# Split weights of the first expert block, unread PE products and a tail in halves: one change to a hybrid encoder layer with a mixture of experts

## The reference

```python
def finish_layer(x, p, o_attn, c, lp):
    ...
    x = x + mixed
    h = rms_norm(x, lp['g_ffn']).reshape(B * T, D)
    idx, wts = hier_route(h, lp['w_coarse'], lp['b_coarse'], lp['w_fine'], lp['b_fine'])   # 2 of 32 experts
    x = x + moe_ffn(h, idx, wts, lp['w_e_gate'], lp['w_e_up'], lp['w_e_down']).reshape(B, T, D)
    gate = jax.nn.sigmoid(rms_norm(x, lp['g_ple']) @ lp['w_ple_gate'])
    return x + gate * (p @ lp['w_ple_proj'])

# moe_ffn: rows are sorted by expert into blocks of 128; for each block xb of expert e
return (jax.nn.silu(xb @ w_g[e]) * (xb @ w_u[e])) @ w_d[e]
```

## Time and profile before

| | us |
|---|---|
| runs | 1288.11, 1289.12, 1291.49 |
| median | 1289.12 |
| the profiled execution, its own time | 1287.65 |
| its span from the first to the last instruction | 1285.9 |
| PE busy | 1218.7 (95%) |
| DVE busy | 958.7 (75%) |
| ACT busy | 716.3 (56%) |
| POOL busy | 411.0 (32%) |

### The profile page before, as it was taken

One profiled execution on the slowest core, in us unless ns is written; L12 is line 12 of the kernel. 1 busy time (PEld: TensorE's weight loads), 2 busy tenths in 40 slices (PEclk: granted clock), 3 DMA queues, 4 the chain that ended last, 5 costly groups with the idle time before them and its releaser, 6 DMA issues.

```text
span 1285.9 us, 18156 instructions
## 1 busy us (share of the span) xinstructions
PE 1218.7 (95%) x6291; PEld 1015.9 (79%) x6291; DVE 958.7 (75%) x966; ACT 716.3 (56%) x881; POOL 411.0 (32%) x397
## 2 busy tenths in 40 slices
PE   6999988899999999779999999999999999996997
PEld 5887977788788888468888888888888888865886
DVE  5223957788783324879999999999999999975652
ACT  4223325655571221447788777787777777763221
POOL 1000016665141000124554445544455444530000
PEclk9999998999999999989999999999999999998999
DMA  7831001000243220289999999999999999955421
GB/s 257 170 65 37 1 17 61 31 28 1 96 174 130 82 74 29 95 331 368 384 369 384 379 370 364 372 391 380 383 398 389 395 411 403 397 215 196 164 99 49
DMA packets 79487, 287.44 MB, mean 224 GB/s; under 512 B 32848, under 2 KB 35600, under 8 KB 54094
## 3 DMA queue, kind: packets, MB, share of 16 engines
q1 hardware_dynamic: 69214, 268.93, 56.3%
q0 software_dynamic: 10224, 17.85, 3.7%
HBM read 275.60 MB, written 30.60 MB: 238 GB/s over the span
## 4 chain that ended last, share of the span: by engine, by line
PE 54%; DVE 3%; DMA 2%; issue 1%; ACT 1%; POOLq 0%; POOL 0%; SPq 0%; DVEq 0%; ACTq 0%
PE ps L462 16%; PE ps L464 16%; PE ps L463 16%; PE ps L1911 4%; DMA mem<-in_w_e_gate 1%; DVE whl L443 1%; PE ps L2196 1%; PE ps L1918 1%; DMA y_rows<-mem 0%; DMA mem<-y_rows 0%; ACT whl L1220 0%; PE ps L2267 0%; DVE mem L1751 0%; DVE mem L1859 0%; DVE mem L1858 0%
## 5 line engine op out<-in xcount | busy, mean ns | idle before, releaser
L443 DVE TENSOR_TENSOR whl<-mem,whl 128x2048 fp32r<-128x2048 f32 (+2 forms) x216 | 489.5, 2268 | 36.2 <-ACT whl L1220 29.7
L462 PE MATMUL ps<-whl,ahl 128*128 128x512 f32 x1136 | 451.3, 397 | 7.3 <-DVE ahl L443 5.7
L1220 ACT ACTIVATE whl<-mem 128x2048 fp32r<-128x2048 f32 x202 | 387.5, 1919 | 100.0 <-PE ps L464 93.8
L464 PE MATMUL ps<-whl,ahl 128*128 128x512 f32 x1136 | 439.7, 387 | 0.0
L463 PE MATMUL ps<-whl,ahl 128*128 128x512 f32 x1136 | 438.9, 386 | 0.0
L462 PEld LDWEIGHTS ps<-whl,ahl 128*128 128x128 f32 x1136 | 216.7, 191 | 49.4 <-DVE whl L443 3.4
L464 PEld LDWEIGHTS ps<-whl,ahl 128*128 128x128 f32 x1136 | 215.7, 190 | 44.0
L463 PEld LDWEIGHTS ps<-whl,ahl 128*128 128x128 f32 x1136 | 216.3, 190 | 39.8
L892 POOL DMA_INDIRECT y_rows<-mem x35 | 93.8, 2681 | 299.0 <-DVE mem L1805 298.2
L777 POOL TENSOR_SCALAR mem<-mem 128x1 f32<-128x1 f32 (+2 forms) x68 | 20.5, 301 | 396.5 <-ACT mem L968 363.8
L968 ACT ACTIVATE mem<-mem 128x1024 bf16<-128x1024 f32 (+1 forms) x54 | 49.1, 909 | 162.1 <-DVE mem L1702 97.2
(11 more groups left out here) (227 smaller groups left out, 1314.9 us busy)
## 6 DMA issues: line engine op xcount, KB each, us to landing
mem<-in_w_e_gate SPq DMA_DIRECT2D x66, 1024.0 KB, 7.6
mem<-in_w_e_up SPq DMA_DIRECT2D x66, 1024.0 KB, 7.6
mem<-in_w_e_down SPq DMA_DIRECT2D x66, 1024.0 KB, 7.9
mem<-in_x_prompt SPq DMA_DIRECT2D x24, 512.0 KB, 3.5
mem<-y_rows SPq DMA_DIRECT2D x16, 512.0 KB, 5.1
mem<-in_w_in SPq DMA_DIRECT2D x4, 1024.0 KB, 11.8
mem<-in_w_out SPq DMA_DIRECT2D x4, 1024.0 KB, 6.4
h_rows<-mem SPq DMA_DIRECT2D x8, 512.0 KB, 2.6
```

The costliest lines, as they stand in the source:

```text
L443: return which.tensor_tensor(out, full, hi.bitcast(F32), ALU.subtract)
L462: nc.tensor.matmul(out, act_hi, whl[:, 0, w_at], start=first, stop=False)
L464: return nc.tensor.matmul(out, act_lo, whl[:, 0, w_at], start=False, stop=last)
L1220: nc.scalar.activation(whl[:, 0, slot * CH:(slot + 1) * CH], raw[c], ACT.Copy).then_inc(s_mhi, jobs)
```

## The change

Six parts:

1. The high halves of the first expert's four chunks move forward in ACT's queue, around the two exponentials; their low halves move from DVE to POOL, ahead of POOL's first gathers.
2. SP loads chunks 0 to 3 of the second expert between the PLE stores and not behind them.
3. Three of DVE's instructions for the table of spilled blocks (`eb`) move ahead of its wait for the second selection product; the others of that table move behind the index tables. Two buffers change place.
4. `ple_project(4)` moves between the two selection products.
5. PE gets products of the unit matrix by itself into bank 7, which nobody reads (`idle_products`): 19 ahead of the first `slots_turned`, 9 behind it, 26 behind the last expert block and 8 behind the first `x2_transpose`.
6. The last tile of the gate stage is done in two halves of 512 columns: PE makes the whole first half before the second, and tanh, the two DVE products and the store follow by halves.

```diff
@@ SP
             for t in range(Q0, NT):
                 if t + 2 < NT:
                     load_p(t + 2)
                 r = rows_of(t)
+                if t == NT - 3:
+                    load_expert_chunk(1, 1, job(0, 1) + 1)
                 sp.wait_ge(s_convs, 1 + 2 * (t - Q0) + 2)
                 sp.dma_start(Q[t * P:t * P + r], q_out[0:r]).then_inc(s_uos, 16)
+                if t in (Q0 + 1, NT - 3, NT - 2):
+                    c = {Q0 + 1: 0, NT - 3: 2, NT - 2: 3}[t]
+                    load_expert_chunk(1, c, job(0, c) + 1)
...
-            for c in range(4):
-                load_expert_chunk(1, c, job(0, c) + 1)
...
+            for h in range(2):
+                at = slice(h * C, (h + 1) * C)
+                sp.wait_ge(s_3f, NT + h)
+                sp.dma_start(o["y_sample"][0][:, at], fin[TS % 2][0:SAMPLE, at]).then_inc(s_out[TS % 2], 16)
@@ POOL
+            for c in range(4):
+                pool.wait_ge(s_mhi, c + 1)
+                at = slice(c * CH, (c + 1) * CH)
+                lo_part(nc.gpsimd, whl[:, 1, at], whl[:, 0, at], raw[c]).then_inc(s_mlv, 3 if c == 3 else 1)
@@ ACT
+            act.wait_ge(s_w, NT)
+            expert_hi(0, 0, 0, 16, None)
+            act.wait_ge(s_rta, 1)
+            nc.scalar.activation(eqc, dc, ACT.Exp).then_inc(s_rta, 1)
+            expert_hi(1, 1, 1, 16, None)
+            p_turned(2)
+            projected(0)
+            act.wait_ge(s_rta, 3)
+            nc.scalar.activation(e2, mt, ACT.Exp).then_inc(s_rta, 1)
+            expert_hi(2, 2, 2, 16, None)
+            p_turned(3)
+            projected(1)
+            expert_hi(3, 3, 3, 16, None, 3)
...
-            act.wait_ge(s_w, NT)
-            for c in range(4):
-                expert_hi(c, c, c, 16, None, 3 if c == 3 else 1)
-                if c < 2:
-                    p_turned(c + 4)
-                if c < 3:
-                    projected(c + 2)
+            for i in range(2, NQ):
+                if i + 2 < NQ:
+                    p_turned(i + 2)
+                projected(i)
             slots_hi(0, 1)
-            projected(NQ - 1)
...
+            for h in range(2):
+                act.wait_ge(s_3g, NT + h)
+                nc.scalar.activation(tg[TS % 2][:, h * C:(h + 1) * C], bank(2 + 2 * (TS % 2) + h), ACT.Tanh, scale=0.5).then_inc(s_3th, 1)
@@ DVE
+            chain(tt(r3(eb, NE), rowof(start, NOVF), j16, ALU.is_le))
+            chain(tt(r3(eb2, NE), rowof(end, NOVF), j16, ALU.is_gt))
+            chain(tt(eb, eb, eb2, ALU.mult))
             dve.wait_ge(s_rtp, 3)
...
-            expert_lo(0, 0, 0)
             slots_lo(0, 1)
-            expert_lo(1, 1, 1)
-            expert_lo(2, 2, 2)
-            expert_lo(3, 3, 3, 3)
             slots_lo(1, 2)
             gated(1)
             dve.sem_inc(s_hl, 1)
+            dve.wait_ge(s_mlv, 6)
...
+                if t == TS:
+                    dve.wait_ge(s_out[t % 2], 16 * (t // 2))
+                    for h in range(2):
+                        at = slice(h * C, (h + 1) * C)
+                        dve.wait_ge(s_3th, t + h + 1)
+                        nc.vector.scalar_tensor_tensor(tg[t % 2][:, at], tg[t % 2][:, at], 1.0, projected_rows[:, at], ALU.add, ALU.mult).then_inc(s_3m, 1)
+                        dve.wait_ge(s_3m, t + h + 1)
+                        nc.vector.scalar_tensor_tensor(fin[t % 2][:, at], tg[t % 2][:, at], 0.5, R[:, t, at], ALU.mult, ALU.add).then_inc(s_3f, 1)
@@ PE
+            def idle_products(b, n):
+                for i in range(n):
+                    nc.tensor.matmul(bank(b, P), ident, ident, start=(i == 0), stop=(i == n - 1))
...
             for k in range(2):
+                if k == 1:
+                    ple_project(4)
                 pe.wait_ge(s_rt, 3 + k)
...
-            ple_project(4)
             ple_project(5)
             pe.wait_ge(s_tab, 1)
             pe.wait_ge(s_convs, 1 + 2 * (NQ - 1))
+            idle_products(7, 19)
             slots_turned(0, 16, None)
+            idle_products(7, 9)
             pe.wait_ge(s_xsl, 1)
...
+            pe.wait_ge(s_convs, 1 + 2 * NQ + 2)
+            idle_products(7, 26)
...
             x2_transpose(0)
+            idle_products(7, 8)
```

More of the change, by code:

```diff
@@ L187, in build_step @@
         rel = take(NE)
+        eb2 = take(NOVF * NE)
         assert top[0] <= HB0
@@ L191, in build_step @@
         V[0] = take(NT * 2 * NBLK)
-        eb, eb2 = (mem[:, HB0 + i * NOVF * NE:HB0 + (i + 1) * NOVF * NE] for i in range(2))
         assert top[0] <= HT0
@@ L196, in build_step @@
         cmp16 = take(NOVF)
+        eb = take(NOVF * NE)
         assert top[0] <= TAIL
@@ L674, in _, with load_expert_chunk @@
                 sp.dma_start(raw_view(c), expert_chunk(0, c)).then_inc(s_mraw[c], 16)
+            def load_expert_chunk(e, c, lo_before):
+                sp.wait_ge(s_mlv, lo_before)
+                sp.dma_start(raw_view(c), expert_chunk(e, c)).then_inc(s_mraw[c], 16)
             for n in range(2 * NT + 2, 3 * NT):
@@ L758, in _ @@
                     q = t - 3
[L759 to L763, removed]
+                    if q < TS:
+                        sp.wait_ge(s_3f, q + 1)
+                        sp.dma_start(o["y_prompt"][0, q * P:(q + 1) * P], fin[q % 2]).then_inc(s_out[q % 2], 16)
+            for h in range(2):
+                at = slice(h * C, (h + 1) * C)
+                sp.wait_ge(s_3f, NT + h)
+                sp.dma_start(o["y_sample"][0][:, at], fin[TS % 2][0:SAMPLE, at]).then_inc(s_out[TS % 2], 16)
+            sp.wait_ge(s_out[0], 16 * 6)
             sp.wait_ge(s_out[1], 16 * 4)
@@ L1204, in _ @@
                     square_sum(R[:, t, :], junk_of(x1_junk, D), ss1, s_hs)
[L1206 to L1213, removed]
             def expert_hi(J, slot, c, arrived, used, jobs=1):
@@ L1330, in _ @@
                     x2_square(t + 3)
-            act.wait_ge(s_3g, NT)
             act.wait_ge(s_3f, NT - 2)
-            nc.scalar.activation(tg[(NT - 1) % 2], banks2(2 + 2 * ((NT - 1) % 2)), ACT.Tanh, scale=0.5).then_inc(s_3th, 1)
+            for h in range(2):
+                act.wait_ge(s_3g, NT + h)
+                nc.scalar.activation(tg[TS % 2][:, h * C:(h + 1) * C], bank(2 + 2 * (TS % 2) + h), ACT.Tanh, scale=0.5).then_inc(s_3th, 1)
         @block.vector
@@ L1755, in _, with expert_lo @@
                 nc.vector.tensor_tensor(Vv[:, :, 1, :], r3(oh, NBLK), over(wk[k], NBLK), ALU.mult).then_inc(s_rt, 1)
+            def expert_lo(J, slot, c, jobs=1):
+                dve.wait_ge(s_mhi, J + 1)
+                at = slice(slot * CH, (slot + 1) * CH)
+                lo_part(nc.vector, whl[:, 1, at], whl[:, 0, at], raw[c]).then_inc(s_mlv, jobs)
+            j16 = over(iota[:, 0:NOVF], NE)
+            chain(tt(r3(eb, NE), rowof(start, NOVF), j16, ALU.is_le))
+            chain(tt(r3(eb2, NE), rowof(end, NOVF), j16, ALU.is_gt))
+            chain(tt(eb, eb, eb2, ALU.mult))
             dve.wait_ge(s_rtp, 3)
@@ L1767, in _ @@
             nc.vector.tensor_copy(wtab, wts).then_inc(s_tab, 1)
[L1769 to L1782, removed]
             def slots_lo(b, count):
@@ L1805, in out_right @@
                 nc.vector.tensor_scalar(y[:, C:2 * C], bank(6), w_cur[b], None, ALU.mult).then_inc(s_y1, 1)
-            expert_lo(0, 0, 0)
+            chain(tt(r3(eb, NE), r3(eb, NE), rowof(iota[:, 0:NE], NOVF), ALU.mult))
+            chain(red(cmp16, r3(eb, NE), AX.X, ALU.add))
+            chain(nc.vector.tensor_copy(ebk.bitcast(I32), cmp16))
+            nc.vector.tensor_copy(novf.bitcast(I32), end[:, NE - 1:NE]).then_inc(s_tab, 1)
             slots_lo(0, 1)
-            expert_lo(1, 1, 1)
-            expert_lo(2, 2, 2)
-            expert_lo(3, 3, 3, 3)
             slots_lo(1, 2)
@@ L1881, in add_ple @@
                     projected_rows = qb[t % 2]
+                if t == TS:
[6 more added lines that the diff above has]
+                        nc.vector.scalar_tensor_tensor(fin[t % 2][:, at], tg[t % 2][:, at], 0.5, R[:, t, at], ALU.mult, ALU.add).then_inc(s_3f, 1)
+                    return
                 nc.vector.scalar_tensor_tensor(tg[t % 2], tg[t % 2], 1.0, projected_rows, ALU.add, ALU.mult).then_inc(s_3m, 1)
@@ L2405, in _ @@
                     hi, lo = act_tile(t % 2, k)
-                    for i in range(2):
+                    for i in range(2 if t < TS else 1):
                         last = split_product(bank(2 + 2 * (t % 2) + i), hi, lo, slice(k * D + i * C, k * D + (i + 1) * C), k == 0, k == KD - 1)
                 last.then_inc(s_3g, 1)
+            for k in range(KD):
+                hi, lo = act_tile(TS % 2, k)
+                last = split_product(bank(3 + 2 * (TS % 2)), hi, lo, slice(k * D + C, (k + 1) * D), k == 0, k == KD - 1)
+            last.then_inc(s_3g, 1)
 _INS = ['x_prompt', 'x_sample', 'p_prompt', 'p_sample', 'cache_k', 'cache_v', 'state_conv', 'g_mix', 'w_in', 'g_q', 'g_k',
```

3 lines of the change are left out of this document (removed).

## The result

The changed kernel takes 1298.37 us (median of 9 runs, 1292.69 to 1302.66) against 1289.12 us before (9 runs, 1286.62 to 1293.42): a ratio of 1.006, 95% interval 1.0038 to 1.0082. It is slower, by 9.25 us; the forecast was 1298.6.

What follows compares the result with a forecast made beforehand. PE bounds the expert loop; around it, DVE's routing chain and PE's waits decide. Terms 17.0 − 0.3 + 0.65 − 6.0 + 0 − 1.8 = +9.5 us on 1287.65, plus 1.5 for the median: 1298.6; range 1284 to 1305.

Steps and rivals of the forecast that it cites:

- The lock: In the routing, POOL's four 2048-column subtractions, 4.6 us each, hold DVE's two-operand instructions to their end: +17.0 us.
- likeliest case: Whole kernel: POOL's subtractions hold DVE's routing for their whole length; +9.5 us in all, median 1298.6, own range 1292 to 1305.
- Selection products: Two selection products with a PLE product now between them: first at low clock, second at full clock; net −0.3 us.
- First turns: Ahead of the first gathered rows' transposes, PLE product plus 19 idle products fill 7.9 us where 7.24 was: +0.65 us.
- rival 3: DVE is held and idle products run at 1.2 GHz: +4 us ahead of first transposes, +2 at end; 1304, chance 0.12.
- First gate and second block: Expert loop's start: earlier loads −2.6 us, clock kept at first gate −1.7 and at second −1.7; together −6.0.
- Behind the last expert: Idle products in PE's wait after the last expert: −2.4 us if the clock lives, +2.3 if not; taken as 0.
- the case of the lost clock: After the last expert the clock is lost, and the 8 idle products behind the turns run 3.4 us: +2.3 us.
- Tail: Last tile in halves: shorter tanh and two DVE products, −1.5 us, and a half-size store; −1.8 us in all.
- Rival 1: DVE is not held through POOL's long subtractions; copies on ACT delay PE by 1.6 us: −5.9 us, 1283, chance 0.18.
- Rival 4: Half of each POOL subtraction falls on DVE instructions it doesn't hold: +8.5 us instead of 17, 1290, chance 0.11.

Runs made afterwards that it cites:

- e4: Changed kernel with POOL's four subtractions over 1024 columns each, the second half of each low half left out; 1288.50 us in one run.
- e1: Changed kernel with the first expert's low halves back on DVE and the second expert's loads back behind the PLE stores; 1282.74 us, ratio 0.9942 to before.
- e2: Kernel before with only parts 1 and 2 of the change put in; 1305.17 us, ratio 1.0123 to before.
- e7: e6 with idle products resized: 16 for 19, 9 more ahead of the loop, 40 for 26, 4 for 8; 1278.16 us, ratio 0.9907 to before.
- e3: Changed kernel with POOL filling the four chunk buffers with zeros where it subtracted, first expert's low halves left out; 1292.03 us in one run.
- e6: e1 with the second expert's first chunk loaded ahead of the last PLE store, the next three right behind it; 1278.74 us, ratio 0.9913 to before.
- e5: Changed kernel without its four groups of idle products; 782.32 us from last logits to span's end, where the changed kernel has 783.14.
- e8: Changed kernel with POOL copying the first expert's four chunks where it subtracted; 767.72 us from last logits to span's end, changed kernel 783.14.

## Why the prediction was right, point by point

**The lock.** The likeliest case held. Predicted +17.0 us, measured 15.3 (the four DVE rows, 15.98, less the 0.69 that they take alone); 15.10 to the gather. Price: 4.50 us where 4.6 was taken. The Trainium skill (GPSIMD Engine Reference, "3.1 Elementwise — side-by-side cycle accounting") gives 4497 ns for an addition of 2048 columns of two fp32 inputs; the 4.50 us of this case's subtraction agree with it. The rest of the difference is that the holds begin 0.2 to 0.4 us after POOL's rows, and the first, whose instruction came that late, 1.3 us after it. The order of the holds, on the four instructions named, was as worked out. The Trainium skill's rule that the lock is kept for the whole instruction (SBUF — State Buffer, "🔬 SBUF: two separate sides") is borne out for 1024 and 2048 columns by e4 and the changed kernel. The prediction found no pair longer than 256 columns before the change; one of 2048 stood there, with the engines the other way round (timelines of POOL and of DVE before):

```profile
545.57 2.47 POOL L905 CAST mem<-mem 128x1 int32<-128x1 f32 x2
```

```profile
545.59 2.28 DVE L443 TENSOR_TENSOR whl<-mem,whl 128x2048 fp32r<-128x2048 f32 x1
```

The same two casts take 0.32 us in the changed kernel, where DVE does nothing beside them.

**Selection products.** Predicted −0.3; 15.10 − 15.3 = −0.2. The first ran at the low level (4.16 us, 3.55 was taken), the second at full clock (2.14).

**First turns.** Predicted +0.65, measured 8.75 − 8.35 = +0.40. The products ran at full clock there, so rival 3 fell.

**First gate and second block.** Predicted −6.0, measured −4.16 − 1.06 = −5.2. The −2.6 and the −1.7 of the first gate product (9 × 0.2, which is 1.8) stood (−4.16); of the 1.7 at the second gate 1.06 came, since the stand of 2.21 us did lose the clock, only for six passes instead of twelve.

**Behind the last expert.** Predicted 0; *start* and *stage* make 0.92 − 1.47 = −0.55. The products that follow the turns ran late by 0.92 us, as the case of the lost clock said, but brought the clock up.

**Tail.** Predicted −1.8, measured 4.85 − 6.99 = −2.14, within the bounds.

**Not seen.** *PLE* grew by 2.17 us: the transfer of the projection's weights was issued as long before its use as in the kernel before, and landed 0.85 us later, and behind a stand of 2.77 us PE ran at the low level. No single part of the change makes it: e1 and e2, which have no edit in common, both show it (10.62 and 10.63), as do five others of the eight; e7 has 9.07. Whether the 8.76 of the one profile of before was chance stays open. This miss, and the 0.8 us at the second block, stand against the 1.7 us by which the lock was put too high and some 1 us of smaller terms; the sum, +9.5 predicted and +9.83 measured, is closer than its terms, and that is luck. So is 1298.37 against 1298.6: the median of the kernel before itself moved from 1289.12 to 1291.92 between sessions.

**Rival 1** fell by the profile, and was mis-sized besides (e3): it took PE's delay to come from ACT's copies, but in e3 it came from the second expert's load, which part 2 puts ahead of a PLE input; the prediction looked only at the row stores behind that load. **Rival 4** fell: the four holds met the instructions on which they were expected, and only 0.2 to 0.4 us of three of POOL's rows, and 1.3 us of the first, went by before DVE stood.

## What to carry to other kernels

In these runs an elementwise instruction of POOL that reads SBUF (the memory in which `mem`, `raw` and `whl` lie; `ps` is another) cost DVE nearly its whole length (4.2 to 4.3 of 4.50 us, 2.1 of 2.35, 1.65 of 1.89) where DVE's next instruction took two operands from SBUF; beside a chain of small DVE instructions that sets the end, four such subtractions cost 15 us though DVE got 9 us of work less (4 × 2.28). In such a place give POOL work that only writes (e3), or leave the work on DVE where DVE waits anyway (e1). And before work is moved to free a buffer sooner, see whether the load that wants the buffer merely stands too late in its queue: e6 got the 3.0 us by moving it.

## What the runs showed of the hardware that was not expected

The prediction did not tell POOL's instructions apart by what they read. POOL's fill of 2048 columns (1.80 us) held no DVE instruction, its copy of 2048 columns (1.89 us) did (1.65 us where 0.18 is usual), and its subtraction of as many columns takes 4.50 us, 2.4 times the copy.

A stand of PE doesn't lose the clock by its length alone: after 2.21 us ahead of the second block the clock fell as soon as PE resumed in the changed kernel (0.67 of full clock in 585.0 to 585.5), and the same four turns ran at full clock in e5 (0.75 us against 1.13).

```profile
585.00:585.50 0.50, 0.39 (x2) 0.39 (x3) 0.50 (x2) 0.50 (x1) 0.00 (x0) 0.67 0.00 0
```

Nor does a fast start show that the clock was kept. In e8, behind the same stand, the turns of 570.05 have 0.74 us, but seven products from 571.67 on run at the low level, 0.63 us each where two before them have 0.39 and 0.40; e2 does the same. Of the seven kernels with this stand only e5 kept the clock throughout, and why is open.

```profile
571.67 0.63 PE L464 MATMUL ps<-whl,ahl 128*128 128x512 f32 x1
```
